# Retention's gate scaled in PSUM, and the second memory layer's norm and key transposes placed anew

## The reference, cut to what matters

```
o = retention(rotary(q, positions), rotary(k, positions), v)
mu = jnp.mean(o, -1, keepdims=True)
var = jnp.mean(jnp.square(o - mu), -1, keepdims=True)
o = ((o - mu) * lax.rsqrt(var + NORM_EPS)).reshape(B, S, TOK_WIDTH) * norm_g.astype(jnp.float32)
...
branch = jnp.concatenate([tok, mem_out.astype(tok.dtype)], -1) * jax.nn.silu(z)
y = branch @ w_out[i]
x = layer_norm(DEEPNORM_ALPHA * x + y, ln_g[i], ln_b[i])
...
kv = mem @ w_kv
mk = kv[..., :MEM_WIDTH].reshape(B, N_MEM, MEM_HEADS, MEM_HEAD_DIM)
```

## Time and profile before

| | |
|---|---|
| median of 3 runs | 2926.92 us (2924.23 to 2928.47) |
| profiled execution, its own time | 2937.41 us |
| profiled execution, span of the core | 2935.6 us |
| PE busy, of the span | 98% |
| POOL busy | 80% |
| ACT busy | 46% |
| DVE busy | 41% |

### The profile page before, as it was taken

The page is one execution under the profiler, slowest core; times in us unless marked ns, Lnnn a source line. Parts: engine busy times, 40 slices in busy tenths (PEclk is TensorE's granted clock), DMA queues, the critical chain, the costliest instruction groups (busy, mean ns, idle before and its releaser), DMA issues.

```text
span 2935.6 us, 40528 instructions
## 1 busy us (share of the span) xinstructions
PE 2867.0 (98%) x13819; PEld 2406.5 (82%) x13819; DVE 1205.2 (41%) x2325; ACT 1364.8 (46%) x1783; POOL 2344.0 (80%) x1831
## 2 busy tenths in 40 slices
PE   9989999999979999999999999999999999999998
PEld 7878788888868888888888888788887888888886
DVE  5253343434442433334333345486535332332334
ACT  4444444444434554544546354555435444444444
POOL 8978898888877665757667588788887999999997
PEclk9999999999999999999999999999999999999999
DMA  8545555555654444434444356444554655655553
GB/s 285 190 161 182 165 191 190 180 188 178 209 180 135 144 143 134 147 122 154 140 138 145 117 172 203 157 140 153 196 164 163 200 194 188 200 186 192 197 193 132
DMA packets 284353, 502.72 MB, mean 171 GB/s; under 512 B 18021, under 2 KB 68662, under 8 KB 283190
## 3 DMA queue, kind: packets, MB, share of 16 engines
q1 hardware_dynamic: 275606, 482.55, 50.0%
q10 hardware_dynamic: 8608, 18.24, 1.7%
HBM read 498.61 MB, written 2.12 MB: 171 GB/s over the span
## 4 chain that ended last, share of the span: by engine, by line
POOL 51%; issue 25%; PE 23%; POOLq 1%; DVE 0%; DVEq 0%; ACT 0%
POOL wlo L418 51%; PE acc L474 8%; PE acc L475 8%; PE acc L476 8%; POOLq L416 0%; POOLq L413 0%; DVE x_sb L2316 0%; POOLq L418 0%; DVE big L2292 0%; DVE kv L1808 0%; DVEq L154 0%; ACT small L1427 0%; DVE small L2283 0%; POOL eps_sb L412 0%; DVE small L2309 0%
## 5 line engine op out<-in xcount | busy, mean ns | idle before, releaser
L418 POOL TENSOR_TENSOR wlo<-raw,whi 128x512 fp32r<-128x512 f32 x1824 | 2343.5, 1317 | 574.5 <-ACT whi L1050 558.2
L1050 ACT ACTIVATE whi<-raw 128x1024 fp32r<-128x1024 f32 x910 | 957.5, 1060 | 1102.6 <-PE acc L476 1058.1
L474 PE MATMUL acc<-whi,a_lo 128*128 128x512 f32 x2528 | 1002.9, 397 | 37.5 <-DVE kv L1773 19.4
L476 PE MATMUL acc<-whi,a_hi 128*128 128x512 f32 x2528 | 988.7, 391 | 0.0
L475 PE MATMUL acc<-wlo,a_hi 128*128 128x512 f32 x2528 | 987.6, 391 | 0.0
L474 PEld LDWEIGHTS acc<-whi,a_lo 128*128 128x128 f32 x2528 | 477.4, 189 | 135.7 <-DVE kv L1773 19.9
L476 PEld LDWEIGHTS acc<-whi,a_hi 128*128 128x128 f32 x2528 | 476.5, 189 | 101.0
L475 PEld LDWEIGHTS acc<-wlo,a_hi 128*128 128x128 f32 x2528 | 477.4, 189 | 95.5
L474 PE MATMUL acc<-whi,b_lo 128*128 128x512 f32 x928 | 365.6, 394 | 0.0
L476 PE MATMUL acc<-whi,b_hi 128*128 128x512 f32 x928 | 361.4, 389 | 0.0
L475 PE MATMUL acc<-wlo,b_hi 128*128 128x512 f32 x928 | 361.2, 389 | 0.0
(11 more groups left out here) (291 smaller groups left out, 2103.2 us busy)
## 6 DMA issues: line engine op xcount, KB each, us to landing
raw<-in_w_in_ret SPq DMA_DIRECT2D x176, 512.0 KB, 4.4
raw<-in_w_in_gdn SPq DMA_DIRECT2D x176, 512.0 KB, 4.3
raw<-in_w_out SPq DMA_DIRECT2D x160, 512.0 KB, 4.5
raw<-in_w_mlp_in SPq DMA_DIRECT2D x128, 512.0 KB, 4.3
raw<-in_w_mlp_out SPq DMA_DIRECT2D x128, 512.0 KB, 4.4
raw<-in_w_in SPq DMA_DIRECT2D x80, 512.0 KB, 4.6
raw<-in_w_mem_kv SPq DMA_DIRECT2D x63, 512.0 KB, 4.8
cb<-log_decays ACTq DMA_DIRECT2D x6, 512.0 KB, 5.6
```

The lines of the kernel that those rows point to most:

```text
L418: part = pool.tensor_tensor(wlo[q % 4][:, c], raw_half[:, c], whi[q % 4][:, c].bitcast(f32), ALU.subtract)
L474: pe.matmul(dst, l, w_h, start=start and block == 0, stop=False)
L476: mm = pe.matmul(dst, h, w_h, start=False, stop=stop and block == KB - 1)
L1050: act.activation(whi[q % 4][:, :], raw[j][:, (q % 2) * HALF:(q % 2 + 1) * HALF], ACT.Copy).then_inc(hi_ready, 1)
```

## The change

It has two parts.

In `ret_end` the mean and the inverse deviation are applied together, in place in PSUM (`(b - mean) * inverse`, four instructions of 128x256), and then the gate is multiplied in with one instruction of 128x512 a head, from PSUM and `zs` into `br`. Before, the order was mean and gate from PSUM into `br`, then the scaling in place in `br` in SBUF.

Between the layers, ACT's root moves from the place after unit `U_KV1 + 1` to unit `U_KV1`, ahead of its half 5. On DVE, the first `keys` moves from behind the layer norm's four chunks to the place behind its third.

```diff
@@ scalar engine, between the layers
             half(U_KV1, 4)
             chunk_mem(3)
+            layer_norm(0)
             for q in range(5, 8):
                 half(U_KV1, q)
 
-            kv_slots(U_KV1, W_KV1, lambda: layer_norm(0), "x1", gates_loaded, gates_hi)
+            kv_slots(U_KV1, W_KV1, lambda: None, "x1", gates_loaded, gates_hi)
@@ vector engine
-            def by_chunks(chunk, part=None):
+            def by_chunks(chunk, part=None, after={}):
 
                 for c in range(4):
                     chunk(c)
+                    if c in after:
+                        after[c]()
@@ ret_end
                 for h in range(2):
+                    b, _ = full("ret", f"o{h}", g)
+                    for t in range(TT):
+                        n, c = 2 * h + t, slice(t * SEQ, (t + 1) * SEQ)
+                        ts(b[:, c], b[:, c], small[:, 24 + 2 * n:25 + 2 * n], small[:, 40 + n:41 + n], SUB, MUL)
+                dve.drain()
+                for h in range(2):
                     b, done = full("ret", f"o{h}", g)
-                    for t in range(TT):
-                        n, c = 2 * h + t, slice(t * COL + h * SEQ, t * COL + (h + 1) * SEQ)
-                        last = stt(out=br[:, c], in0=b[:, t * SEQ:(t + 1) * SEQ], scalar=small[:, 24 + 2 * n:25 + 2 * n], in1=zs[:, c],
-                                   op0=SUB, op1=MUL)
-                    last.then_inc(done, 1)
-                dve.drain()
-                for h in range(2):
-                    for t in range(TT):
-                        n, c = 2 * h + t, slice(t * COL + h * SEQ, t * COL + (h + 1) * SEQ)
-                        last = ts(br[:, c], br[:, c], small[:, 40 + n:41 + n], None, MUL)
-                last.then_inc(s["branch_ready"], 1)
-                dve.drain()
+                    to = br.rearrange("p (t c) -> p t c", t=TT)[:, :, h * SEQ:(h + 1) * SEQ]
+                    z = zs.rearrange("p (t c) -> p t c", t=TT)[:, :, h * SEQ:(h + 1) * SEQ]
+                    tt(to, b[:, :].rearrange("p (t c) -> p t c", t=TT), z, MUL).then_inc(done, 1)
+                dve.drain().then_inc(s["branch_ready"], 1)
@@ vector engine, between the layers
-            layer_norm(0)
-            keys(U_KV1, W_KV1, 0)
+            layer_norm(0, None, {2: lambda: keys(U_KV1, W_KV1, 0)})
             keys(U_KV1, W_KV1, 1)
```

More of the change, by code:

```diff
@@ L1879, in ret_end @@
                 for h in range(2):
-                    b, done = full("ret", f"o{h}", g)
+                    b, _ = full("ret", f"o{h}", g)
                     for t in range(TT):
-                        n, c = 2 * h + t, slice(t * COL + h * SEQ, t * COL + (h + 1) * SEQ)
-                        last = stt(out=br[:, c], in0=b[:, t * SEQ:(t + 1) * SEQ], scalar=small[:, 24 + 2 * n:25 + 2 * n], in1=zs[:, c],
-                                   op0=SUB, op1=MUL)
-                    last.then_inc(done, 1)
+                        n, c = 2 * h + t, slice(t * SEQ, (t + 1) * SEQ)
+                        ts(b[:, c], b[:, c], small[:, 24 + 2 * n:25 + 2 * n], small[:, 40 + n:41 + n], SUB, MUL)
                 dve.drain()
                 for h in range(2):
-                    for t in range(TT):
-                        n, c = 2 * h + t, slice(t * COL + h * SEQ, t * COL + (h + 1) * SEQ)
-                        last = ts(br[:, c], br[:, c], small[:, 40 + n:41 + n], None, MUL)
-                last.then_inc(s["branch_ready"], 1)
-                dve.drain()
+                    b, done = full("ret", f"o{h}", g)
+                    to = br.rearrange("p (t c) -> p t c", t=TT)[:, :, h * SEQ:(h + 1) * SEQ]
+                    z = zs.rearrange("p (t c) -> p t c", t=TT)[:, :, h * SEQ:(h + 1) * SEQ]
+                    tt(to, b[:, :].rearrange("p (t c) -> p t c", t=TT), z, MUL).then_inc(done, 1)
+                dve.drain().then_inc(s["branch_ready"], 1)
                 turn_out("ret", g, br)
@@ L2171, in layer, with layer_norm @@
                 dve.drain()
-            def layer_norm(i, part=None):
+            def layer_norm(i, part=None, after={}):
                 for t in range(TT):
@@ L2190, in chunk @@
                             op0=MUL, op1=ADD).then_inc(s["x_final"], 1)
-                by_chunks(chunk, part)
+                by_chunks(chunk, part, after)
             def scale_x():
```

## The result

The changed kernel took 2902.44 us, the median of 4 runs (2899.47 to 2905.03); the kernel before, run beside it, 2927.69 (2924.23 to 2930.03). The ratio is 0.9914, 95% interval 0.9897 to 0.9932: 25.3 us, or 0.86%, faster. The forecast was 2888.5, its range 2882 to 2902, so the gain is real and the time lies just above the range. In the two profiled executions the difference is larger: 2903.09 against 2937.41, 34.3 us. The 2937.41 is not among the runs whose median is given.

The account below looks back on a forecast made before the run. PE, busy 98% of the span, was taken as the bound. Retention waits -19.5, the `kv` wait -20.9 and delays beside the norm +1.9 sum to -38.5 us; from the median 2926.9 that gives 2888.5, range 2882 to 2902.

Parts of the forecast that it names:

- The sum's starting point: Whole kernel: the summed gain of 38.5 us was taken from the runs' median, 2926.9, not the profiled 2937.4, giving 2888.5.
- The first rival: Retention waits: the timed runs have less of them than the profile, so only 28.0 us can be won, 2898.9; 16%.
- Part one: Retention gate: without the SBUF scaling, PE's waits for POOL near 203 and 303 and their slow starts go, 19.5 us.
- My reading of the mechanism: Retention gate: DVE waits for POOL to run dry, ACT for DVE, POOL for ACT, PE for POOL; the scaling took 14.61 us.
- Part two: Between the layers: early root and `keys` remove PE's `kv` wait and slow start, 20.9 us, at 1.9 us cost.
- The rival by which the norm holds POOL for its whole length: Norm between the layers: each instruction blocks POOL entirely, costing 8.2 us in place of 1.9, so 2894.8; 8%.
- My 0.354: Norm between the layers: each norm instruction delays POOL beside it by 0.354 us; twelve are 4.25 us.
- Starving: Norm between the layers: its instructions need POOL's gaps and finish as late as before, 868.3, giving 2910.5; 5%.
- The slower rival: Gate, all six groups: each of six new instructions waits for a POOL gap, 67 us in place of 19.5, 2955.5; 3%.
- that of a waiting PSUM scaling: Retention gate, two groups: the scaling in PSUM waits for POOL as L1890 did, giving 2907.9; 4%.

Follow-up runs that it names:

- e4: The changed kernel run again without any edit; 2899.23 us median of 5 runs, ratio 0.9885 to the kernel before.
- e1: The kernel before, unchanged, run and profiled again; 2930.67 us median of 12 runs, ratio 0.9994.
- e5: The changed kernel with both `keys` behind the whole norm as before, only ACT's root early; 2902.54 us, ratio 0.9886.
- e7: The changed kernel with the old gate, its SBUF scaling made an instruction of two SBUF inputs; 2919.99 us, ratio 0.9944.
- e8: The changed kernel with four SBUF scalings by 1.0 of 128x256 added behind the new gate; 2917.46 us, ratio 0.9936.
- e9: The changed kernel with two SBUF instructions of 128x512 in nearly the norm's form added behind the gate; 2921.71 us, ratio 0.9945.

## Why the prediction was wrong

**The sum's starting point failed**, the step "Against the profiled execution's own 2937.4 that gives 2898.9. It was 10.5 us longer than the median of the runs, 2926.9; taken from the median the sum gives 2888.5 us." It took waits measured in one execution, two of them of 8.64 and 6.15 us in retention, away from the time of other executions, which needn't have had them. The first rival said this and gave 2898.9; I gave it 16%, on the ground that 10.5 us "can be the profiler's". The runs show otherwise: a profiled execution of the same kernel took 2920.78, had neither wait, and was the fastest of its 12. The unprofiled runs reach 2943.0, as high as the first profile and higher. How many of the runs of before beside the result (2924.23 to 2930.03) had a wait isn't shown, since they have no trace; that the whole 10.5 us were such waits is therefore argued, not measured.

**The remaining 4 us** are a second, smaller miss. The 2898.9 became 2903.09 in the profiled execution, since 38.2 us of distance shrank to 34.3 on the way to the end, in stretches like that at 1803, after waits that were there before. No term held that. It isn't a fixed price of the change: e4 runs the same program in 2897.23, with a clock of 1.00 from 1790 to 2200 where the first execution has 0.98. 2888.5 + 10.5 + 4.2 is 2903.2, beside 2903.09 for the profiled execution; that is bookkeeping and no proof, since the 4.2 is what that execution left of the 38.5 (38.5 - 34.3).

**Part one** was right where the waits occur: 19.75 us in the trace against 19.5. L1886 takes 0.544 us, against 0.4 to 0.5 forecast, and four with two products 3.2 us, as said; nothing hangs on it. My reading of the mechanism ("the scaling seems to get through only when POOL pauses") holds where a scaling is shut out: each hold ended as POOL ran out of rounded halves. It was too strong as a rule: in e1 the scaling got through beside a running POOL, at about one of its instructions for each of POOL's, and either may happen at the same gate. That was what made part one's worth a matter of the execution.

**Part two** was right: the root at 806.44 after 0.45 us, twelve instructions at 1.63 us (1.67 forecast), no wait for `kv`, and waits for POOL of 1.4 us between 805 and 905 against the 1.9 of the sum, none over 0.4. The rival by which the norm holds POOL for its whole length (8%) gave 8.2 us of cost in its place and falls: there is mutual delay, but POOL's 48 instructions took 66.92 us with sixteen of the norm among them, and at 27.62 / 22 = 1.26 us each in a row with nothing of the kind beside it (the one from 391.55 in the earlier trace rows) they would be 60.3, so a norm instruction cost it 0.42 us and not its own 0.75, and took 1.63 and not 2.05. (My 0.354 was read a little low, since four in 5.20 us isn't POOL's full pace; at 1.26 each the same row gives 0.40.) The rule of the Trainium skill as I applied it, in "SBUF — State Buffer", section "SBUF: two separate sides", is not borne out as a hold for the whole instruction here. Starving (5%) falls as well. One thing I had taken for part of the gain isn't: the keys' new place. e5 does without it, at the same time.

**The slower rival** and that of a waiting PSUM scaling fall with the 24 durations between 539 and 553 ns.

## What to carry to other kernels

A wait taken from one profiled execution may be absent in others of the same program; subtract it only from the time of the execution that had it, and take a second profile before you subtract it from a median. An instruction of VectorE from SBUF to SBUF beside a GpSimd that runs without pause can stand far longer than its neighbours' durations suggest, and it then delays whoever waits for both; working in PSUM for as long as the operand is there avoids it, at 0.2 us an instruction (L1886's 0.544 us; L1890 took 0.34 where nothing held it). What ended such a stand each time was GpSimd's running out of input, so a GpSimd that has a stock of it is the one to watch. If a small result (here a root of 128x2) is queued behind a row of halves that wait for the engine they feed, move it first, and see what it alone brings before other moves are added.

## What the runs showed of the hardware

An instruction of DVE from SBUF to SBUF beside POOL either goes one to each of POOL's instructions, or one of them is shut out through many of POOL's. At group 0 the four scalings of the kernel before took 1.29 to 1.38 us each in e1; where one was shut out it stood 12.2 to 13.9 us, to the end of POOL's row, and those behind it took 0.28 to 0.68 in before, e7, e8 and e9. At group 1 one stood 7.7 to 9.4 us, to the point where POOL had caught up with ACT, and those behind it went one to one (1.2 to 1.8 us) until the row ended. Which of the two happens changes from execution to execution: the same program came to group 0's gate at 175.64 in one and at 175.77 in the other. The long stand was seen at groups 0 and 1 alone, with one input or two in SBUF, with 256 columns or 512, with drains or without. At the four other gates POOL was waiting for ACT's halves; what kept the norm from it is open.

The clock is the second source of scatter. Behind the same 0.86 us wait at the same instruction the granted clock was 0.70 over ten microseconds in one execution of the changed kernel and 0.86 in another, and a mean clock of 0.995 in place of 0.998 goes with 5.0 to 6.5 us of the time in e4's runs.
